# Masked copies of VectorE over half of the columns in a seven-level score scan

## The reference, cut to what matters

```
S_t = diag(f_t) S_{t-1} + k_t v_t^T          f = lb + (1 - lb) * sigmoid(f_raw),  k = 1 - f
o_t = S_t^T q_t
A[t, s] = sum_c q[t, c] * k[s, c] * prod_{s < r <= t} f[r, c]     for s <= t,   o_t = sum_s A[t, s] v_s
```

## Time and profile before

| | |
|---|---|
| median of three runs | 2409.68 us |
| the profiled execution, own time | 2411.77 us |
| its span in the profile | 2409.9 us |
| PE busy | 2278.9 us (95%) |
| DVE busy | 837.4 us (35%) |
| POOL busy | 927.4 us (38%) |
| mean granted PE clock | 0.955 of full |

### The profile page before, as it was taken

How to read it: one execution, slowest core, us unless ns; L and a number is a source line. 1 busy time by engine, 2 the same in 40 slices (tenths; PEclk the granted TensorE clock), 3 DMA queues, 4 the chain that set the end, 5 groups by cost and what they waited for, 6 DMA issues and landing times.

```text
span 2409.9 us, 33460 instructions
## 1 busy us (share of the span) xinstructions
PE 2278.9 (95%) x13221; PEld 1978.2 (82%) x13221; DVE 837.4 (35%) x1288; ACT 755.0 (31%) x1081; POOL 927.4 (38%) x707
## 2 busy tenths in 40 slices
PE   6999999998799889999999899999988999999997
PEld 5888887786688667888787899999988689899886
DVE  4222103113555362222106422232149245555401
ACT  4333213122566523233314432212100323334311
POOL 3444444330412133444444344444434103544542
PEclk9999999997899989999999999999999869999999
DMA  4322322340000022232322222222210002232221
GB/s 148 98 93 87 105 87 88 96 142 18 1 1 1 8 71 88 88 104 88 104 87 87 71 87 87 88 98 90 84 43 1 18 1 88 88 99 92 90 102 61
DMA packets 150735, 179.53 MB, mean 74 GB/s; under 512 B 6925, under 2 KB 140398, under 8 KB 150654
## 3 DMA queue, kind: packets, MB, share of 16 engines
q1 hardware_dynamic: 150491, 178.35, 22.9%
q10 hardware_dynamic: 163, 0.04, 0.0%
HBM read 176.28 MB, written 2.10 MB: 74 GB/s over the span
## 4 chain that ended last, share of the span: by engine, by line
PE 55%; issue 25%; POOL 11%; DVE 6%; ACT 1%; SPq 1%; DMA 0%; POOLq 0%; DVEq 0%; ACTq 0%
PE ps L1520 35%; POOL wlo L614 11%; PE ps L1652 10%; PE ps L1981 2%; PE ps L1873 1%; PE ps L1847 1%; DVE Ad L1430 1%; PE ps L1777 1%; PE ps L1859 1%; DVE Q L1447 1%; PE ps L1766 1%; DVE tmp L1029 0%; PE ps L1869 0%; PE ps L1845 0%; DVE Tod L1453 0%
## 5 line engine op out<-in xcount | busy, mean ns | idle before, releaser
L614 POOL TENSOR_TENSOR wlo<-raw,whi 128x512 fp32r<-128x512 f32 x638 | 834.7, 1340 | 1200.5 <-ACT whi L693 1200.5
L1520 PE MATMUL ps<-xh,whi 128*128 128x512 f32 (+2 forms) x2432 | 700.8, 334 | 21.0 <-POOL wlo L614 12.2
L1520 PE MATMUL ps<-xh,wlo 128*128 128x512 f32 (+2 forms) x2432 | 701.7, 335 | 0.0
L1520 PE MATMUL ps<-xl,whi 128*128 128x512 f32 (+2 forms) x2432 | 701.0, 334 | 0.0
L693 ACT ACTIVATE whi<-raw 128x2048 fp32r<-128x2048 f32 x160 | 304.7, 1905 | 757.4 <-PE ps L1520 440.2
L1520 PEld LDWEIGHTS ps<-xh,whi 128*128 128x128 f32 x2432 | 417.4, 190 | 71.3 <-POOL wlo L614 10.7
L1520 PEld LDWEIGHTS ps<-xl,whi 128*128 128x128 f32 x2432 | 416.1, 190 | 46.2
L1520 PEld LDWEIGHTS ps<-xh,wlo 128*128 128x128 f32 x2432 | 414.8, 190 | 46.4
L1652 PE MATMUL ps<-act_l,whi 128*128 (+1 forms) x528 | 208.6, 395 | 0.0
L1652 PE MATMUL ps<-act_h,wlo 128*128 (+1 forms) x528 | 208.6, 395 | 0.0
L1652 PE MATMUL ps<-act_h,whi 128*128 (+1 forms) x528 | 208.6, 395 | 0.0
(11 more groups left out here) (307 smaller groups left out, 2639.4 us busy)
## 6 DMA issues: line engine op xcount, KB each, us to landing
raw<-in_w_in SPq DMA_DIRECT2D x47, 1024.0 KB, 5.0
raw<-in_ffn_wg SPq DMA_DIRECT2D x22, 1024.0 KB, 5.3
raw<-in_ffn_wu SPq DMA_DIRECT2D x22, 1024.0 KB, 5.3
raw<-in_ffn_wd SPq DMA_DIRECT2D x22, 1024.0 KB, 4.9
raw<-in_w_up SPq DMA_DIRECT2D x22, 1024.0 KB, 5.1
raw<-in_w_down SPq DMA_DIRECT2D x11, 1024.0 KB, 4.8
raw<-in_w_out SPq DMA_DIRECT2D x8, 1024.0 KB, 5.2
raw<-in_ple_w_gate SPq DMA_DIRECT2D x4, 1024.0 KB, 5.1
```

The lines of the kernel that those rows point to most:

```text
L614: last = nc.gpsimd.tensor_tensor(wlo[:, slot, d], raw[:, slot, d], whi[:, slot, d].bitcast(F32), ALU.subtract)
L1520: last = mm(ps[:, j * banks + b, 0:n], w[:, k, e * P:(e + 1) * P], x[:, k, c0:c0 + n], start=(k == 0 and q == 0), stop=(k == KD - 1 and q ...
```

## The change

At levels 0 to 6 the copy takes only the columns of second halves: destination, mask and source are all viewed as (tile, pair, half, position), and half 1 is taken. That is 256 columns in place of 512, in runs of w = 1, 2, 4, ... 64 words with gaps of the same width. The copies of level -1 and of the meta tokens, every product on PE and every other instruction stay as they were.

```
-                    elif lv < 7:
+                    elif 0 <= lv < 7:
+                        second = lambda x: x.rearrange("p (i b e w) -> p i b e w", i=TT, e=2, w=1 << lv)[:, :, :, 1, :]
+                        mask = levelmask[:, lv + 1, :].rearrange("p (b e w) -> p b e w", e=2, w=1 << lv)[:, :, 1, :]
+                        nc.vector.copy_predicated(second(Ad[:, n, :]), mask.unsqueeze(1).to_broadcast([P, TT, HD >> lv, 1 << lv]),
+                                                  second(ps[:, bank, :])).then_inc(lev_sel, 1)
+                    elif lv < 0:
                         nc.vector.copy_predicated(Ad[:, n, :].rearrange("p (i t) -> p i t", i=TT),
                                                   levelmask[:, lv + 1, :].unsqueeze(1).to_broadcast([P, TT, P]),
                                                   ps[:, bank, :].rearrange("p (i t) -> p i t", i=TT)).then_inc(lev_sel, 1)
```

## The result

The changed kernel takes 2396.78 us, the median of 5 runs (2396.18 to 2397.91), beside 2409.68 for the kernel before (2408.76 to 2411.94, 5 runs). The ratio is 0.9946 with an interval of 0.9932 to 0.9961. The profiled execution took 2396.59 us with a span of 2394.8.

A forecast was written before the change was run, and what follows sets the result against it. It took DVE, held by its lock with POOL's K updates, as the levels' bound, PE right behind. Terms 0 + 1.2 + 2.3 + 1.1 + 0 + 1.4 = 6.0 us off 2409.7 gave 2403.7, range 2399.0 to 2408.8.

The forecast's parts named there:

- levels 0, 1: First two levels: Q updates and T product still wait for K updates, PE at half clock hides the rest; gain 0.
- level 2: Group g0: Q update comes ahead of the K update, PE starts level 3 earlier; gain 1.2 us, otherwise 0.7 or 3.0.
- level 4: T product ends in front of the next K update, so PE goes on without a gap; gain 2.3 us.
- levels 5, 6: PE's starts on four more groups come 3.67 us apart in place of 3.95; gain 1.1 us.
- clock in the levels: Three half-clock falls stay, the last two at other moments and 0.7 us cheaper each; gain 1.4, bounds 3 either way.
- behind the levels: After the last Q update everything shifts with it, and shorter copies tell on nothing more; no further gain.
- 19.2 + 2.7 = 21.9 us in 13 waits: PE's idle time in the levels ended by DVE's T product, taken as the most faster copies can give at full clock.
- The forecast of 0.454 at all levels: Time in us of one masked copy of half the columns, 721 - 267 ns; bounds 0.72 and 0.36.
- The rival built on that rule: Single-word steps are dear at level 0 alone: copy 0.83 us, about 3.5 us gained, 2406.2; chance 0.10.
- give the levels' gain back: T products of levels 2 and 4 still meet K updates, only 1.1 us is left: 2408.6; chance 0.22.
- nothing became slower: Rival: short PSUM runs cost at levels 0 to 3, at three times a column 5.2 us slower, 2414.9; chance 0.08.
- the pass-through of all 15.0 us: Rival: DVE is busy throughout the levels, so all its saved time comes off: 2394.7; chance 0.03.

The follow-up runs named there:

- lv01: The changed kernel with narrow copies at levels 0 and 1 alone, levels 2 to 6 copying all 512 columns; 2411.13 us, ratio 1.0004.
- late117: The changed kernel with two added DVE products, 1.2 us in all, between the last level and the output stage; 2404.50 us.
- fill_before: The kernel before with constant identity products added on PE where it waits in the levels; 2400.78 us, ratio 0.9959.
- fill: The changed kernel with constant identity products added on PE where it waits in the levels; 2397.14 us, ratio 0.9955.
- nok_before: The kernel before with each K update of POOL cut to one column a head; 2396.43 us in one run.
- fillhoist: The changed kernel with level 0's T products moved ahead of the first copies and constant products in PE's waits; 2398.35 us, ratio 0.9944.
- dst: The changed kernel with mask bytes packed and copy destinations written side by side, only PSUM still stepped; 2399.14 us in one run.
- late3_before: The kernel before with three added DVE products, 2.5 us in all, between the last level and the output stage; 2410.47 us.
- compact: The changed kernel with PE computing only the 64 target columns a tile, side by side in PSUM; 2428.47 us, ratio 1.0081.
- pack: The changed kernel with the mask bytes of the target columns packed side by side; 2397.05 us, ratio 0.995.

## Why the prediction was half right

The direction, what bounds the levels (DVE and its lock with POOL) and the path through them were right; the gain was over twice the sum. Step by step, from PE's start on level -1:

| step | forecast | measured | how |
|---|---|---|---|
| levels 0, 1 | 0 | 0 | start on level 2 at 32.00, now 31.98; lv01 |
| level 2 | 1.2 | 1.1 | start on level 3 at 44.77, now 43.65 |
| level 4 | 2.3 | 2.4 | start on level 5: 4.7 earlier in all, 1.2 of it the clock behind level 2 |
| levels 5, 6 | 1.1 | 1.3 | start on level 7 at 80.86, now 74.8 |
| clock in the levels | 1.4 | 3.1 to 3.9 | below |
| behind the levels | 0 | 4.8 | 524.8, now 520.0; late117 |
| sum (with 3.1 for the clock) | 6.0 | 12.8 | 12.9 over the medians |

**Right.** The path through the levels, place by place. The four terms without the clock make 4.6. At nearly full clock in both kernels, fill_before and fill, the levels differ by 96.1 - 91.8 = 4.3. Groups are 3.62 apart in place of the 3.67 forecast, Q updates of levels 4 to 6 took 1.95 to 2.08 where about 1.9 was forecast, and the list of PE's waits for the T product fell to 14.7 us where 15 were forecast. Of DVE's time 6.4 us went (91.07 to 84.64), less than the 15.0 taken off by the copies on paper, because the holds of Q updates and the slow copies of levels 0 and 1 took the rest.

**A bound that was misread: "19.2 + 2.7 = 21.9 us in 13 waits".** This counts PE's products and weight loads as if they waited one after the other. The products waited 10.1 us and the loads 11.7, mostly at the same time, so about that, and not 21.9, is what faster copies could give at full clock in these levels. The forecast's own terms were stepped from the timeline and don't rest on it.

**The step that failed first: "the last two fall at other moments, and halfway between 1.4 and 2.8 is 0.7 cheaper each: 1.4".** That term was mis-sized. The low stretch behind level 2 gave 1.2, from 10.26 to 9.04. The other low stretch did not become cheaper, it went: before, it lay in the products of levels 7 and 8, and is gone, though the wait ahead of them is nearly the same (3.33 and 3.10 us); from PE's start on level 7 to its start on the outputs are 1.9 us less than before. Before's own levels lose 3.9 to the clock by fill_before. The changed kernel's lose 0.2 by fill, since there DVE is late anyhow. The prediction named 3 us either way as its bound. Even with 3 more, and with level 2 at its best (3.0 in place of 1.2), the gain would be 10.8, still 2.1 short of 12.9: the rest is the next step.

**The step that failed most: behind the levels "everything shifts with it".** Work does shift: no instruction there waits for something new. But the output stage runs at a granted clock of 0.72 to 0.77 in every run here, so a good part of its time is half-clock time, and how much depends on the moment at which it is reached. The prediction had the clock at 0.52 in one wait of the levels and never asked for it behind them. A window over the stage would have shown 0.72 over 81.4 us, which is 45 us at half clock: a stage that can move by several us without any change to its work. This is shown by late117 (+1.2 us of work, +7.7 us), by nok_before and fill_before (wide copies, 77.9 and 77.4 for the stage), and by fillhoist (narrow copies, 81.4). It also means that some 4.8 of the 12.9 us belong to this kernel and this arrival, and not to narrow copies as such.

**A wrong size that cost nothing: the copies of levels 0 and 1.** The forecast of 0.454 at all levels holds for levels 2 to 6 (0.432). At level 0 the copies took 0.818, and at level 1 0.774. The prediction's argument from the Q update of level 0, which reads and writes every second word at full rate, doesn't carry over to a masked copy. In the Trainium skill's "Vector Engine (DVE) Microarchitecture Reference", section "Measured stream behaviour on trn2", single words with small steps lose rate, and the estimate of 0.83 us from it is what level 0 shows (0.818). The section allows full rate to runs of two adjacent words; the trace disagrees at level 1, so the agreement at level 0 may be chance. dst shows that at least the destination has to be stepped. The rival built on that rule gave 2406.2; its copy time came true, and its effect on the path did not: in a row such copies lose nothing against the wide ones (2.55 for 2.63 us), and lv01 lost nothing.

**The rivals.** The lock didn't give the levels' gain back (no stall at level 4), nothing became slower, and the pass-through of all 15.0 us (2394.7) came near in the total by accident only: the levels' 8.0 hold 3 to 4 of clock, and 4.8 came from behind them.

What stays open: what makes a moment of arrival good or bad beyond the cases measured, how often one kernel meets each (all but fillhoist's scatter rests on one profile a kernel), and why late3_before gained 1.5 behind its levels and not more.

## What to carry to other kernels

Where two engines lock each other out, a shorter instruction ahead of the lock is worth what PE's next start gains, found by stepping the few instructions to the next start; here that gave 4.6 for 4.3. Then take the windows of every stage behind the change and look at the granted clock: a stage below full clock can give or take some us, 6 here, merely by being reached 1 us sooner or later, so a time alone can't judge an edit in front of it, and the stages have to be compared one by one. Before a masked copy is narrowed, look at its destination: with runs of one or two words one copy of half the columns took longer than one of all, and four in a row saved 0.1 us. And a list of what a line waited for has to be asked for one engine at a time before its sums are used.

## What the runs showed of the hardware

- A masked copy of 256 columns takes 0.43 us with destination runs of four words or more (levels 2 to 6) or a destination side by side (0.44), and 0.77 to 0.82 with runs of two or one. All 512 take 0.72. Four in a row take 1.42 to 1.44, 2.44 to 2.55 and (512 columns) 2.54 to 2.63. A Q update over 1024 columns with every second word on both sides takes 1.23 before, so not every stepped write is slow.
- Half the moving columns on PE were not half the time, but half the clock. In compact, 64 products of 64 columns took 13.91 us, and the levels ran at 0.63. At level 0, still at full clock, a weight load took 192 ns as with 128 columns. From level 1 on PE was busy for 87.8 of 88.9 us, and the clock stayed at half all the same, at level 6 too, where the moving columns come in runs of 64 adjacent words; so the steps in them are not what kept it low. compact also has PE write adjacent words of PSUM, and no run tells that from the number of columns. The clock rose while the products of level 7 ran, which have 128 columns again:

```profile
1805.10 13.91 PE L2011 MATMUL ps<-Q,K 128*128 128x64 f32 x64 [3.76 <-DVE Tod L1458]
...
L2011 PEld LDWEIGHTS ps<-Q,K x448: 186/333/338, 1793.3 to 1889.0; 128*128 128x128 f32 x150
...
1784.10:1906.50 122.40, 114.20 (x657) 111.77 (x657) 93.80 (x117) 7.84 (x16) 42.30 (x20) 0.63 0.01 1
...
1804.00:1892.90 88.90, 87.80 (x449) 87.22 (x449) 65.95 (x93) 1.15 (x3) 24.60 (x12) 0.50 0.00 1
```

  The weight loads set the pace of these products: 192 ns each at full clock in the changed kernel, a median of 333 here. Sparing PE columns that nobody reads cost 32 us.
- The output stage, in which PE is busy 97% of the time with many small products, never ran at full clock as a whole: 0.72 to 0.77 in each of 18 profiles, its length 77.2 to 81.5 us.
- Half-clock stretches were reproducible. lv01 and the kernel before, whose products of the levels start at the same distances from the first, have 23.5 us each of them in the levels and 62 behind; the changed kernel and pack 13.2 and 49 each.
